# A transformer block in split float32 on one Trainium2 core: mixer scores one unit later, squares, fold and low parts rearranged at the output projection, the local query's high part and the masks' load moved

## What is computed

```python
# first block: mixing branches, cross attention, SwiGLU
h = rms_norm(x, mix_norm_g)
(c_b, c_c, c_u, f_q, f_k, f_v, f_g, s_q, s_k, s_v, gates) = split_proj(h @ w_in)
merged = gate0 * (conv @ wb0) + gate1 * (fox @ wb1) + gate2 * (swa @ wb2)   # s_q: local (windowed) query
x = x + merged @ w_mix_out
x = x + cross_attention(rms_norm(x), rms_norm(mem), ...)                    # keys and values from mem
x = x + swiglu(rms_norm(x), ...)
x = rms_norm(x, final_norm_g)
# second block: bidirectional recurrence ("mixer"), spatial gating, output projection, FFN
z = rms_norm(x) @ w_in_2            # zq, zf (two directions), zi, zg, zu, zv, ga, gb
a_out = hgrn2_mixer(zq, zf_f, zf_b, zi, zg, ...)
b_out = spatial_gating(zu, zv, ...)
merged = sigmoid(ga) * (a_out @ w_a) + sigmoid(gb) * (b_out @ w_b)
x = x + rms_norm(merged @ w_out, norm_mix_post)
x = x + rms_norm(swiglu(rms_norm(x), ...), norm_ffn_post)
x = x + (p @ w_ple) * sigmoid(x @ w_ple_gate)
```

## Time and profile before

| | us |
|---|---|
| median of 3 runs | 1088.25 |
| lowest and highest run | 1087.6, 1090.77 |
| the profiled execution's own time | 1089.45 |
| its span, first to last instruction | 1087.7 |
| PE busy | 1074.7 (99% of the span) |
| PEld busy | 960.4 (88%) |
| DVE busy | 751.3 (69%) |
| ACT busy | 602.7 (55%) |

### The profile page before, as it was taken

The page is one execution under the profiler, slowest core; times in us unless marked ns, Lnnn a source line. Parts: engine busy times, 40 slices in busy tenths (PEclk is TensorE's granted clock), DMA queues, the critical chain, the costliest instruction groups (busy, mean ns, idle before and its releaser), DMA issues.

```text
span 1087.7 us, 16240 instructions
## 1 busy us (share of the span) xinstructions
PE 1074.7 (99%) x6880; PEld 960.4 (88%) x6880; DVE 751.3 (69%) x897; ACT 602.7 (55%) x731; POOL 0.2 (0%) x4
## 2 busy tenths in 40 slices
PE   9999999999999999999999999999999999999998
PEld 8888777789998988888889899999999888888887
DVE  5465855466745478776568897679947888776557
ACT  5543365543535455555446985589555675554443
POOL 0000000000000000000000000000000000000000
PEclk9999999999999999999999999999999999999999
DMA  9963244565553556564655455443544646664651
GB/s 281 244 215 117 78 155 145 149 209 186 169 188 117 155 184 215 191 194 146 212 182 180 133 156 166 144 156 117 155 155 146 193 155 195 193 194 155 196 172 39
DMA packets 141448, 183.08 MB, mean 168 GB/s; under 512 B 14132, under 2 KB 91936, under 8 KB 141376
## 3 DMA queue, kind: packets, MB, share of 16 engines
q1 hardware_dynamic: 141160, 181.85, 52.8%
q10 hardware_dynamic: 216, 0.21, 0.1%
HBM read 180.79 MB, written 1.25 MB: 167 GB/s over the span
## 4 chain that ended last, share of the span: by engine, by line
PE 91%; ACT 4%; DVE 3%; issue 1%; DVEq 0%; ACTq 0%
PE ps L543 28%; PE ps L569 22%; PE ps L600 14%; PE ps L571 11%; PE ps L987 2%; PE ps L1116 2%; PE ps L646 1%; DVE wlo L1753 1%; PE ps L806 1%; ACT whi L1169 1%; PE ps L781 1%; PE ps L648 1%; PE ps L793 1%; PE ps L876 1%; PE ps L1002 1%
## 5 line engine op out<-in xcount | busy, mean ns | idle before, releaser
L1753 DVE TENSOR_TENSOR wlo<-raw,whi 128x2048 fp32r<-128x2048 f32 (+3 forms) x170 | 378.4, 2228 | 173.1 <-ACT whi L1169 172.6
L1169 ACT ACTIVATE whi<-raw 128x2048 fp32r<-128x2048 f32 (+1 forms) x167 | 310.5, 1863 | 89.9 <-PE ps L571 36.2
L543 PE MATMUL ps<-ha,whi 128*128 128x256 f32 x1328 | 243.1, 285 | 4.3 <-DVE wlo L1753 4.3
L569 PE MATMUL ps<-ha,whi 128*128 128x512 f32 x640 | 226.2, 399 | 0.6 <-DVE wlo L1753 0.6
L543 PEld LDWEIGHTS ps<-ha,whi 128*128 128x128 f32 x1328 | 206.9, 192 | 8.2 <-issue 7.1
L543 PE MATMUL ps<-ha,wlo 128*128 128x256 f32 x664 | 187.8, 283 | 0.0
L571 PE MATMUL ps<-ha,wlo 128*128 128x256 f32 x640 | 179.4, 280 | 0.0
L569 PEld LDWEIGHTS ps<-ha,whi 128*128 128x128 f32 x640 | 120.2, 188 | 30.6 <-issue 0.9
L543 PEld LDWEIGHTS ps<-ha,wlo 128*128 128x128 f32 x664 | 127.2, 192 | 0.0
L569 PE MATMUL ps<-pr,whi 128*128 128x512 f32 x352 | 124.5, 399 | 0.0
L571 PEld LDWEIGHTS ps<-ha,wlo 128*128 128x128 f32 x640 | 120.8, 189 | 0.1
(11 more groups left out here) (381 smaller groups left out, 1691.7 us busy)
## 6 DMA issues: line engine op xcount, KB each, us to landing
raw<-in_w_in SPq DMA_DIRECT2D x54, 1024.0 KB, 5.3
raw<-in_w_ffn_gate SPq DMA_DIRECT2D x11, 1024.0 KB, 5.1
raw<-in_w_ffn_up SPq DMA_DIRECT2D x11, 1024.0 KB, 5.2
raw<-in_w_gate SPq DMA_DIRECT2D x11, 1024.0 KB, 5.1
raw<-in_w_up SPq DMA_DIRECT2D x11, 1024.0 KB, 5.1
raw<-in_w_xkv SPq DMA_DIRECT2D x8, 1024.0 KB, 5.1
raw<-in_w_ffn_down SPq DMA_DIRECT2D x8, 1024.0 KB, 5.0
raw<-in_w_down SPq DMA_DIRECT2D x8, 1024.0 KB, 5.0
```

The costliest lines, as they stand in the source:

```text
L543: mm = e.matmul(ps[0:width, m * T:(m + 1) * T], a[:, kk, m * width:(m + 1) * width], b[:, off + k, :], start=k == 0 and j == 0 and m % 2 = ...
L569: e.matmul(banks[s][:, at_:at_ + 512], wh[:, kk, c], H[2][:, :, k, :], start=k == 0, stop=False, skip_group_check=True)
L1169: e.activation(h, r, ACT.Copy).then_inc(*hi_done.up(n))
L1753: e.tensor_tensor(l, r, h.bitcast(F32), ALU.subtract).then_inc(*lo_done.up(n))
```

## The change

Five edits, none of which adds or removes work of PE, ACT or the DMA queues, but for their order.

1. SP issues the load of the masks behind the last load of `cc` instead of between the two units of `sq`, and DVE casts them behind the taps of the convolution instead of before the first attention head.
2. ACT makes the first unit of `sq` high before the memory's norm (`rs_tm`), the second one behind it as before.
3. PE does the scores of each level of the first mixer (i = 0) one weight unit later; `hq1` and `ff1` take in the last ones. ACT and DVE make the two units of `zu` high and low one place earlier; behind that `slot` shifts by one, and ACT evaluates `tanh_q(1)` before `mix_norm(0)`.
4. At the output projection ("post mix" alone) the third square and the third fold come before the next weight unit's high and low part.
5. In `add_normed` (both uses) DVE normalises and adds k + 1 before it makes the low part of k.

```diff
@@ SP
         fetch_for("fk")
-        e.dma_start(mk[:, :, :], d["c_masks"].rearrange("p (l n) -> p l n", l=7)).then_inc(s_mk, 16)
         fetch_for("fv")
...
-        fetch_for("svf", "sq", "cc", "cu", "cb")
+        fetch_for("svf", "sq", "cc")
+        e.dma_start(mk[:, :, :], d["c_masks"].rearrange("p (l n) -> p l n", l=7)).then_inc(s_mk, 16)
+        fetch_for("cu", "cb")
@@ PE
         unit_tm("zv", 1, HA, 3)
-        mixer(0, 1)
-        linear("zu", HA, 0, None, a_stat.on(("ln", "final")), lambda i: mixer(0, 2 + i))
+        linear("zu", HA, 0, None, a_stat.on(("ln", "final")), lambda i: mixer(0, 1 + i))
...
-        linear("zg0", HA, 1, None, a_evac.on(("zi0", 1)), lambda i: mixer(0, 8 + i))
-        unit("hq1", 0, HA, 0, None, a_evac.on(("zi1", 1)))
-        mixer(0, 10)
-        unit("hq1", 1, HA, 0)
+        linear("zg0", HA, 1, None, a_evac.on(("zi0", 1)), lambda i: mixer(0, 7 + i))
+        linear("hq1", HA, 0, None, a_evac.on(("zi1", 1)), lambda i: mixer(0, 9 + i))
+        unit("ff1", 0, HA, 1, None, v_mix.on(("zg", 0)))
         mixer(0, 11)
-        linear("ff1", HA, 1, None, v_mix.on(("zg", 0)))
+        unit("ff1", 1, HA, 1)
@@ ACT
         norm_hi("mem", MN, "mem_norm_g", 3, 1)
+        hi(U["svf"][0][0] + 2)
         e.wait_ge(*pe_sum.on("rows x"))
         rs_tm("mem", m_tm, 20)
-        hi_for("svf")
+        hi(U["svf"][1][0] + 2)
...
         hi(U["hq0"][1][0] + 2)
+        hi(U["zv"][0][0] + 2)
         half_logs(0, 0)
...
         tanh_q(0)
-        hi(U["zv"][0][0] + 2)
+        hi(U["zv"][1][0] + 2)
...
         tanh_zg(0)
         hi(U["hq1"][0][0] + 2)
-        mix_norm(0)
+        mix_scores(0, 8)
         hi(U["hq1"][1][0] + 2)
         e.wait_ge(*v_mix.on(("zg", 0)))
         tanh_q(1)
+        mix_norm(0)
...
+            if square_name == "post mix":
+                square(4)
+                before(3)
@@ DVE
         rows_of("mem", Rm, 3)
-        e.wait_ge(s_mk, 16)
-        e.tensor_copy(masks[:, :, :], mk[:, :, :]).then_inc(*v_stat.up("masks"))
...
+        e.wait_ge(s_mk, 16)
+        e.tensor_copy(masks[:, :, :], mk[:, :, :]).then_inc(*v_stat.up("masks"))
         lo(U["cb"][0][0] + 2)
...
+            if square_name == "post mix":
+                fold_in(2)
+                before(3)
...
-            normed(0)
-            for k in range(8):
+            def added(k):
+                normed(k)
                 e.wait_ge(*v_stat.on(("nh", name, k)))
                 e.tensor_tensor(X[:, k, :], X[:, k, :], nh[:, k, :], ALU.add).then_inc(*v_stat.up((split_name, k)))
+
+            added(0)
+            for k in range(8):
                 if k < 7:
-                    normed(k + 1)
+                    added(k + 1)
                 e.wait_ge(*v_stat.on((split_name, k)))
```

More of the change, by code:

```diff
@@ L1032, in tensor @@
         unit_tm("zv", 1, HA, 3)
-        mixer(0, 1)
-        linear("zu", HA, 0, None, a_stat.on(("ln", "final")), lambda i: mixer(0, 2 + i))
+        linear("zu", HA, 0, None, a_stat.on(("ln", "final")), lambda i: mixer(0, 1 + i))
         for i in range(2):
             unit_tm(f"zi{i}", 0, HA, 1 - i, v_mix.on(("q", 0)) if i == 0 else a_evac.on("zu"))
+            mixer(0, 3 + 2 * i)
+            unit_tm(f"zi{i}", 1, HA, 1 - i)
             mixer(0, 4 + 2 * i)
-            unit_tm(f"zi{i}", 1, HA, 1 - i)
-            mixer(0, 5 + 2 * i)
-        linear("zg0", HA, 1, None, a_evac.on(("zi0", 1)), lambda i: mixer(0, 8 + i))
-        unit("hq1", 0, HA, 0, None, a_evac.on(("zi1", 1)))
-        mixer(0, 10)
-        unit("hq1", 1, HA, 0)
+        linear("zg0", HA, 1, None, a_evac.on(("zi0", 1)), lambda i: mixer(0, 7 + i))
+        linear("hq1", HA, 0, None, a_evac.on(("zi1", 1)), lambda i: mixer(0, 9 + i))
+        unit("ff1", 0, HA, 1, None, v_mix.on(("zg", 0)))
         mixer(0, 11)
-        linear("ff1", HA, 1, None, v_mix.on(("zg", 0)))
+        unit("ff1", 1, HA, 1)
         unit("fb1", 0, HA, 0, None, v_mix.on(("q", 1)))
@@ L1581, in slot @@
             mix_scores(i, t - 1)
-        slot(U["zv"][1][0], 0, 1)
         for k, (u, _, _) in enumerate(U["zu"]):
-            slot(u, 0, 2 + k)
+            slot(u, 0, 1 + k)
         for t_ in range(2):
@@ L1592, in scalar @@
             for k, (u, _, _) in enumerate(U[f"zi{i}"]):
-                slot(u, 0, 4 + 2 * i + k)
+                slot(u, 0, 3 + 2 * i + k)
             evac_tm(f"zi{i}", 1 - i, lambda t_: v[:, t_, 512 * i:512 * i + 512])
@@ L1601, in tanh_zg @@
                 *a_mix.up(("tanh zg", i)))
-        slot(U["zg0"][0][0], 0, 8)
-        hi(U["zg0"][1][0] + 2)
-        mix_scores(0, 8)
+        for k, (u, _, _) in enumerate(U["zg0"]):
+            slot(u, 0, 7 + k)
         tanh_zg(0)
         hi(U["hq1"][0][0] + 2)
-        mix_norm(0)
+        mix_scores(0, 8)
         hi(U["hq1"][1][0] + 2)
@@ L1683, in evac_pieces @@
                 e.activation(mix[:, 2 * g:2 * g + 2, :], split_sums(ss[g])[1], ACT.Copy).then_inc(*a_evac.up((name, g)))
-            before(3)
-            square(4)
+            if square_name == "post mix":
+                square(4)
+                before(3)
+            else:
+                before(3)
+                square(4)
             late()
@@ L2234, in vector @@
         lo(U["hq0"][1][0] + 2)
+        lo(U["zv"][0][0] + 2)
         half_log(0, 0)
@@ L2238, in vector @@
         gated_q(0)
-        lo(U["zv"][0][0] + 2)
+        lo(U["zv"][1][0] + 2)
         def slot(u, i, t):
@@ L2244, in slot @@
             mix_scores(i, t - 1)
-        slot(U["zv"][1][0], 0, 1)
-        for name, t in (("zu", 2), ("zi0", 4), ("zi1", 6)):
+        for name, t in (("zu", 1), ("zi0", 3), ("zi1", 5), ("zg0", 7)):
             for k, (u, _, _) in enumerate(U[name]):
                 slot(u, 0, t + k)
-        slot(U["zg0"][0][0], 0, 8)
-        lo(U["zg0"][1][0] + 2)
-        mix_scores(0, 8)
         def gated_zg(i):
@@ L2365, in add_pieces @@
             fold_in(1)
-            before(3)
-            fold_in(2)
+            if square_name == "post mix":
+                fold_in(2)
+                before(3)
+            else:
+                before(3)
+                fold_in(2)
             late(0)
```

## The result

| | before | after |
|---|---|---|
| median of the four runs timed together, us | 1087.92 | 1079.54 |
| lowest and highest | 1085.44, 1090.77 | 1078.34, 1079.64 |
| the profiled execution, us (its span) | 1089.45 (1087.7) | 1078.34 (1076.5) |

Over all executions the kernel before took 1088.7 in the median (122 of them with their clocks, 1083.6 to 1093.8 but for one at 1096.3), and the changed one 1081.7 (24, 1078.2 to 1085.8), 6.9 us or 0.6% less. So the first four executions of the changed kernel were 2.2 us better than it usually is.

What follows compares the result with a forecast made beforehand. PE, busy 99% of the span, was taken to bound the kernel, so only its waits could be won: 2.77 + 1.0 + 1.3 - 0.1 = 5.0 us, say 4.9, from 1088.25 to 1083.4 us. Range 1081.8 to 1087.0.

Steps and rivals of the forecast that it cites:

- Place A: PE's 2.84 us wait before the first unit of `sq`; making its high part before the memory's norm gains 2.77 us.
- `diagonal` made nobody wait: Narrowest spot before PE's sums: reserve shrinks from 3.4 to 0.8 us; rival of a new wait there, 1085.4 us, chance 0.12.
- Place B: PE's 0.83 us wait before the first unit of `zu` in the first mixer; scores one unit later gain 1.0 us.
- The sums at the end of the mixer: PE's sums one unit later, done at 701; reserve for their roots falls from two us to 1.2, nothing taken.
- the slower rival: First mixer ends a unit late and delays `mix_out` and the second mixer, up to 7.5 us: 1091.7 us; chance 0.06.
- Place C: Output projection to `bg1`, start of the second FFN: 0.29 - 0.15 + 0.35 + 0.8 = 1.3 us won.
- the eight turns: DVE's add-and-normalise loop at the output projection: PE becomes the slower one, 0.35 us won.
- the turn of the loop: DVE's add-and-normalise loop: a turn takes 1.27 us instead of 1.47, no longer going through ACT and back.
- The other use of the loop: Add-and-normalise loop at "post ffn": only the later first low part counts, 0.1 us lost.
- The sum: Whole kernel: 2.77 + 1.0 + 1.3 - 0.1 = 5.0 us, say 4.9; that all three hold, chance 0.62.
- The step from the sum to the time: Whole kernel: the gain taken from 1088.25 us gives 1083.4 us, 0.45% less, since only PE's waits can be won.
- more is won: More stretches where PE is busy but slowed may open with earlier scores: one or two us more, 1081.9; chance 0.08.

Runs made afterwards that it cites:

- f2: Kernel before plus one extra, overwritten 32-column matmul at `au5` and one at `bg2`; median 1087.35 us of 12.
- f1: Changed kernel plus one extra, overwritten 32-column matmul at `au5` and one at `bg2`; median 1079.51 us of 6.
- f4: Changed kernel with extra 32-column matmuls at `au5` and `bg2`, and with edits 4 and 5 undone; median 1083.78 us of 12.
- c1: Kernel before, unchanged, profiled once more; median 1087.78 us of 10.
- c3: Kernel before with edit 5 alone (addition k + 1 ahead of the low part of k); median 1087.65 us of 10.
- e4: Changed kernel, unchanged, profiled a third time; median 1081.76 us of 7.
- d3: Changed kernel with edit 2 undone (memory's norm again ahead of the first high part of `sq`); median 1086.3 us of 12.
- f3: Changed kernel with extra 32-column matmuls at `au5` and `bg2`, and with edit 3 undone (first mixer's scores where they stood before); median 1080.90 us of 8.
- d4: Changed kernel with an extra, overwritten matmul of 0 to 256 columns between units of both FFNs; one execution, no time given.
- e2: Changed kernel plus one extra, overwritten 96-column matmul at `au4` and one at `bg2`; median 1084.31 us of 12.
- e3: Kernel before plus one extra, overwritten 32-column matmul at `au4` and one at `bg2`; median 1089.48 us of 12.
- d1: Changed kernel, unchanged, profiled again; median 1084.34 us of 7, ratio to before 0.996.

## Why the prediction was wrong

*Place A.* Gain 2.77 forecast, 2.73 measured in every pair: right, and `diagonal` made nobody wait. **A step that failed** is the sentence that made it the whole gain. Behind this wait the clock falls in three of four executions, which costs 1.5 us more. The row that it was built on the earlier trace rows came from an execution in which the clock had stayed up, and nothing in that trace could show the other case.

*Place B.* Gain 1.0 forecast, 1.04 to 1.09 measured. The sums at the end of the mixer came in time; the slower rival did not happen.

*Place C.* 1.3 forecast for edits 4 and 5; 1.54 (f2 against f1) and 1.67 (f4 against f1) measured, and 1.35 for edit 5 alone (c1 against c3), where the terms forecast for it make 1.0. From before to after by finer marks: 0.29 at PE's first sum (0.41 to 0.12) and 0.79 at `bg1`, as forecast; 0.05 lost before the first product, where 0.15 was forecast; 0.52 won in the eight turns (0.3 in e4, where the turns themselves ran slower), where 0.35 was. The wait before `bg1` went, and the turn of the loop was right. The other use of the loop lost 0.20 to 0.22, not 0.1: the first `ha` starts 1.72 us behind the first `nh` now at both uses; before, it was 1.59 at the output projection and 1.51 there.

*The sum.* 5.0 us forecast, 5.1 measured with the pace held: the parts were right to 0.4 us each, and that they met to 0.1 is partly luck, since B and C were put too low and A and the gain at the second FFN's end too high. Put against the usual times of both kernels, 6.9 us apart, the forecast misses the clock (1.5 us in 74% of the executions of before and 8% of after, 1.0 us) and 0.8 us that f1 to f4 do not settle: draws, or odds of the pace that the edits shift.

*The step from the sum to the time.* **This step failed too, and it is the larger one.** "So only time in which PE waits can be won", and "It lies 1.2 above the median of the three runs; from 1088.25 the forecast is 1083.4 us", with a range up and down from there, took PE's pace in the FFNs for a constant. It differs between executions of one kernel: by 2.4 us in the first FFN and 3.2 in the second (up to 3.5 with `bg1`). The profiled execution of before had both slow, that of after both fast: 5.5 of the 11.2 us between the two spans, won where PE was 100% busy before and after. The rival "more is won" had the right observation, that PE's busy time is no measure of its pace, and the wrong size and place: one or two us more by earlier scores, where it was 6 us by a pattern of the matmuls themselves. That the three runs of before lay 3.2 us apart was the sign that I passed over: it was read as noise of the measurement, and it was the kernel's own.

What stays open: whether the edits shift the odds of the pace. At `au4`, with the copy as written, the pace was fast in one of five profiles of kernels built on before, and in eight of ten built on the changed one, but these came from different chips in part, and undoing A, B or C (d3, f3, f4) left it fast each time. Behind `bg1` it was fast in two of seven with the wait and in eight of thirteen without. Neither count decides, and the medians of f1, f2 and f4 leave room for it. Open too is what sets the pace inside PE.

## What to carry to other kernels

Cut the traces of several executions of one kernel at the same instruction before you build on one: a stretch that agrees to 0.01 us can be forecast to 0.1, and a stretch with two values needs both in the range. A wait of PE can cost more than its length if the clock falls behind it, so the removal of the longest is worth more than the profile of a lucky execution shows. And a median from a handful of executions can be 2 us off when draws of 2.4 and 3.2 us are in it.

## What the runs showed of the hardware

A row of 512- and 256-column matmuls on fp32r with a weight load for each runs at 346.7 or 353.3 ns a pair, at full clock and without a wait. It keeps its pace over more than 900 matmuls, through other engines' traffic, and changed only where the row is broken: by a matmul of another length (d4), or by a wait of 22 to 33 ns (`au4`). In d4 what a break did went with the pattern before it and with the length of the extra matmul, in both FFNs alike; e2, e3 and f3 show that these two do not settle it. What in PE makes the pattern no run shows.

The granted clock fell to 0.50 behind waits of 2.85 us for about 3.4 us, in five of the six profiles that have this wait (by the mean clock, in 90 of 122 executions of before), and in two profiles behind waits of 1.96 us (d1) and 2.18 us (d3). The Trainium skill ("TensorE: Matmul & The Clock Gate", section "What's actually happening") says that the chip looks at PE's activity on a beat of its own, which does not start with the kernel. The counts here agree: the same wait at the same instant of the program is punished in one execution and not in another.
